# A 31-tap convolution split between VectorE and GpSimd: another order of its parts, and W_out in order of use

## What is computed

```python
z = rms_norm(x, norm1_g) @ w_in                      # 1024 -> 512 pool, 512 value, 512 gate
y_pool = einsum((window_mean(u) - u), pool_lin) * pool_scale   # 4 groups, windows 2, 4, 8, 16
v = a * sigmoid(gate)
h = depthwise_conv(v, width 31) + conv_dw_b          # causal, 512 channels
h = layer_norm(h, ln_g, ln_b);  y_conv = h * sigmoid(h)
x = x + concat(y_pool, y_conv) @ w_out + b_out
x = x + hier_moe(rms_norm(x, norm2_g))               # 32 experts, top 2 in the top group
y = rms_norm(x)
```

## Time and profile before

| | us |
|---|---|
| median of 3 runs (range) | 1133.28 (1131.29 to 1134.9) |
| the profiled execution | 1134.65 |
| its span, first to last instruction | 1132.9 |
| busy: PE | 944.6 |
| busy: DVE | 950.2 |
| busy: ACT | 622.2 |
| busy: POOL | 320.5 |

### The profile page before, as it was taken

How to read it: one execution, slowest core, us unless ns; L and a number is a source line. 1 busy time by engine, 2 the same in 40 slices (tenths; PEclk the granted TensorE clock), 3 DMA queues, 4 the chain that set the end, 5 groups by cost and what they waited for, 6 DMA issues and landing times.

```text
span 1132.9 us, 13497 instructions
## 1 busy us (share of the span) xinstructions
PE 944.6 (83%) x4446; PEld 774.3 (68%) x4446; DVE 950.2 (84%) x965; ACT 622.2 (55%) x596; POOL 320.5 (28%) x292
## 2 busy tenths in 40 slices
PE   4997887377469999497999999999999999999720
PEld 4786766254347887476888888888888888888510
DVE  6289999989987687788988989889898988989338
ACT  7213412116443421374788787878788788787323
POOL 2138969636652110112111111211112111111000
PEclk8998988688689999588999999999999999999865
DMA  8201100103004435268999999999999999999556
GB/s 252 94 20 37 38 19 19 56 1 118 1 19 149 183 115 195 80 230 293 383 380 381 386 383 394 394 388 393 376 391 375 384 379 378 384 382 348 206 233 248
DMA packets 66299, 268.63 MB, mean 237 GB/s; under 512 B 15215, under 2 KB 28015, under 8 KB 40601
## 3 DMA queue, kind: packets, MB, share of 16 engines
q1 hardware_dynamic: 56761, 250.36, 59.3%
q0 software_dynamic: 9504, 17.85, 4.1%
HBM read 254.09 MB, written 30.86 MB: 252 GB/s over the span
## 4 chain that ended last, share of the span: by engine, by line
PE 60%; DVE 25%; issue 3%; ACT 2%; DMA 1%; POOL 0%; DVEq 0%; POOLq 0%; ACTq 0%
DVE arena L1116 16%; PE ps L986 10%; PE ps L984 10%; PE ps L985 10%; PE ps L998 5%; PE ps L999 5%; PE ps L1000 5%; PE ps L973 3%; PE ps L774 2%; PE ps L775 2%; PE ps L776 2%; DVE arena L1424 2%; PE ps L1005 1%; DVE big L1157 1%; PE ps L918 1%
## 5 line engine op out<-in xcount | busy, mean ns | idle before, releaser
L699 ACT ACTIVATE big<-arena 128x2048 fp32r<-128x2048 f32 x192 | 362.6, 1913 | 70.5 <-PE ps L1000 36.4
L1359 DVE TENSOR_TENSOR low<-arena,big 128x2048 fp32r<-128x2048 f32 x126 | 285.1, 2284 | 39.9 <-ACT big L699 37.2
L1116 DVE SCALAR_TENSOR_TENSOR arena<-arena,cols 128x512 f32<-128x512 f32 (+2 forms) x210 | 226.7, 1134 | 1.9
L984 PE MATMUL ps<-big,ring 128*128 128x512 f32 x512 | 204.1, 399 | 2.4 <-DVE ring L1364 2.4
L986 PE MATMUL ps<-big,ring 128*128 128x512 f32 x512 | 202.0, 395 | 0.0
L774 PE MATMUL ps<-big,ring 128*128 128x512 f32 (+2 forms) x432 | 165.6, 383 | 40.5 <-DVE ring L1181 17.1
L1359 DVE TENSOR_TENSOR big<-arena,big 128x2048 fp32r<-128x2048 f32 x66 | 150.9, 2288 | 18.8 <-ACT big L699 15.4
L775 PE MATMUL ps<-big,ring 128*128 128x512 f32 (+2 forms) x432 | 163.3, 378 | 0.0
L776 PE MATMUL ps<-big,ring 128*128 128x512 f32 (+2 forms) x432 | 162.2, 376 | 0.0
L774 PEld LDWEIGHTS ps<-big,ring 128*128 128x128 f32 (+1 forms) x432 | 84.4, 195 | 56.9 <-issue 26.0
L984 PEld LDWEIGHTS ps<-big,ring 128*128 128x128 f32 x512 | 96.8, 189 | 22.0 <-DVE ring L1364 2.8
(11 more groups left out here) (217 smaller groups left out, 1287.2 us busy)
## 6 DMA issues: line engine op xcount, KB each, us to landing
arena<-in_w_eg SPq DMA_DIRECT2D x64, 1024.0 KB, 7.4
arena<-in_w_eu SPq DMA_DIRECT2D x64, 1024.0 KB, 7.0
arena<-in_w_ed SPq DMA_DIRECT2D x64, 1024.0 KB, 7.1
arena<-in_x_prompt SPq DMA_DIRECT2D x16, 512.0 KB, 5.3
y_in<-y_scratch SPq DMA_DIRECT2D x8, 1024.0 KB, 12.2
arena<-in_w_in SPq DMA_DIRECT2D x12, 512.0 KB, 3.5
arena<-in_w_out SPq DMA_DIRECT2D x8, 512.0 KB, 3.7
x_scratch<-arena SPq DMA_DIRECT2D x8, 512.0 KB, 2.8
```

Source lines behind the costliest of these rows:

```text
L699: act.activation(we_h[n % RING], raw[n % RING], ACT.Copy).then_inc(high_done, 1)
L984: pe.matmul(out, part_h[b][:, k, :], wh[:, q, :], start=(k == 0), stop=False)
L1116: dve.scalar_tensor_tensor(hc[:, c, a:b], v_ext[:, c, a + j:b + j], cols[:, c, j:j + 1], hc[:, c, a:b], ALU.mult, ALU.add).then_inc(conv_s ...
L1359: dve.tensor_tensor(we_l[n % RING], raw[n % RING], we_h[n % RING].bitcast(F32), ALU.subtract).then_inc(low_done, 1)
```

## The change

The parts are cut anew. DVE does A of all four tiles first, one after the other, then B of tile 2, B of tile 3 and C of tile 1; C is now the last 206 columns (from CUT = 912). POOL, with ACT's products in three buffers instead of two, adds the 606 later columns of tile 0 and 400 of tile 1, both during the in-projection, and nothing after it. There are three conv_done signals: after the A parts, after B3, after C1. All four pool chunks now stand behind the gate and value chunks.

The window scaling and the difference move from ACT and POOL to DVE, as one instruction per group; POOL's window sums wait for it where they reuse a buffer. The 64-column block of a chunk lies in bank 2 for both sets, so before it PE also waits until the chunk just before was read (taken(j - 1)). The first mean moves from chunk 11 to chunk 10, the first variance into chunk 11. The out-projection of a tile is cut in a half of convolution rows (out_conv) and one of pool rows (out_pool), W_out is loaded and split in that order (WO_ROWS), and the sample tokens of the pool product are a product of their own. PE's order becomes out_conv(0), out_conv(1), out_pool(0), out_pool(1), turn_hm(0), tile 2, the means, turn_hm(1), the variances, logits(0), tile 3. The name run stands for the same slice of hc as before.

```diff
-        KINDS = [("gate", 0), ("value", 0), ("gate", 1), ("value", 1), ("gate", 2), ("value", 2), ("pool", 3),
-                 ("gate", 3), ("value", 3), ("pool", 2), ("pool", 1), ("pool", 0)]
+        KINDS = [("gate", 0), ("value", 0), ("gate", 1), ("value", 1), ("gate", 2), ("value", 2), ("gate", 3),
+                 ("value", 3), ("pool", 3), ("pool", 2), ("pool", 1), ("pool", 0)]
...
-        CUT = HW_ - 220
-        PART = {"A": (0, BANK), "B": (BANK, HW_), "C": (BANK, CUT)}
-        HELPED = [(1, BANK, HW_), (3, CUT, HW_)]
-        help_n = {4: 7, 5: 7, 6: 7, 8: 6, 9: TAPS - 1 - 27}
-        DVE_WO = (0, 1, 4, 5, 6)
+        CUT = BANK + 400
+        PART = {"A": (0, BANK), "B": (BANK, HW_), "C": (CUT, HW_)}
+        HELPED = [(0, BANK, HW_), (1, BANK, CUT)]
+        help_n = {2: (0, 6), 3: (0, 7), 4: (0, 7), 5: (0, 7), 6: (0, 3), 7: (1, 10), 8: (1, 10), 9: (1, 10)}
+        WO_ROWS = list(range(NG, KD)) + list(range(NG))
+        DVE_WO = (0, 1, 2, 3, 4)
...
             for j in range(1, NCH):
                 pe.wait_ge(wl_done, j + 1)
                 if j >= 2:
+                    taken(j - 2)
                 for n in range(3):
+                    if n == 2:
+
+                        taken(j - 1)
                     in_proj(j, n)
...
             pool_lin_product(0)
             pool_lin_product(1)
-            pe.wait_ge(cen_done, 1)
             pe.wait_ge(lnsd_done, 1)
             turn_state(2)
+            pool_lin_product(2)
+            pe.wait_ge(yp_done, 2)
+            pe.wait_ge(wl_dve, NC)
+            out_conv(0)
+            pe.wait_ge(st_done, 3)
             turn_state(3)
-            pool_lin_product(2)
             pool_lin_product(3)
+            pe.wait_ge(yp_dve, 2)
+            pe.wait_ge(st_done, 4)
+            out_conv(1)
+            pe.wait_ge(wl_done, NCH + len(POOL_WO))
+            pe.wait_ge(wl_dve, len(DVE_WO))
+            out_pool(0)
+            pool_lin_sample()
+            out_pool(1)
...
             glu(0)
-            taps(21, ("A", 0), ("B", 0))
+            taps(TAPS, ("A", 0))
             glu(1)
-            taps(TAPS - 21, ("A", 0), ("B", 0))
-            taps(10, ("A", 1))
+            taps(TAPS, ("A", 1))
             glu(2)
-            taps(TAPS - 10, ("A", 1), ("A", 2))
-            taps(10, ("A", 2), ("B", 2))
+            taps(TAPS, ("A", 2))
             glu(3)
             taps(TAPS, ("A", 3))
...
+            taps(9, ("B", 2))
+            ln_center(0)
+            taps(5, ("B", 2))
+            difference(0)
+            taps(7, ("B", 2))
+            difference(1)
+            taps(8, ("B", 2))
+            difference(2)
+            taps(2, ("B", 2))
+            ln_normal(0)
+            for k in range(4):
+                wo_low(k)
+            mix_conv_low(0)
+            difference(3)
+            pooled(2)
+            mix_conv_low(1)
+            wo_low(4)
+            pooled(3)
+            mix_pool_low(0)
+            mix_pool_low(1)
+            taps(10, ("B", 3))
...
+                if t == 0:
+                    pooled_sample()
+                    taps(TAPS - 10, ("B", 3))
+                    dve.wait_ge(conv_step, steps[0])
+                    dve.engine_nop().then_inc(conv_done, 1)
+                    taps(10, ("C", 1))
                 if t == 1:
-                    mix_low(t + 2)
-                    ln_center(1)
-                    ln_center(2)
+                    taps(TAPS - 10, ("C", 1))
+                    dve.wait_ge(conv_step, steps[0])
+                    dve.engine_nop().then_inc(conv_done, 1)
```

More of the change, by code:

```diff
@@ L660, in hm_turned @@
                 act.activation(hmT[:, :, 0:ROWS[t]], x_ps[:, :, 0:ROWS[t]], ACT.Copy).then_inc(hmT_done, 1)
+            ln_swish(0)
+            mix_conv_high(0)
+            pooled(1)
+            mix_conv_high(1)
+            state_rows(2)
+            wo_high(4)
+            wo_high(5)
+            state_rows(3)
+            wo_high(6)
+            wo_high(7)
             act.wait_ge(yp_dve, NG - 2)
-            mix_high(0)
-            mix_high(1)
+            for t in (0, 1):
+                act.activation(part_h[t][:, 0:NG, :], u_ext[:, :, t * P:(t + 1) * P], ACT.Copy).then_inc(mh_done, 1)
             act.wait_ge(st_out, 64)
-            products(1, TAPS)
             for t in range(NT):
@@ L814, in ln_mean, with ln_variance @@
                 ins.then_inc(mean_done, 1)
+            def ln_variance(n):
+                w = BLOCKS[n][1]
+                pe.wait_ge(sq_done, n + 1)
+                for c in range(NC):
+                    ins = pe.matmul(var_ps[n][:, 0:w], mean_w[:, :], sq[n][:, c, 0:w], start=(c == 0), stop=(c == NC - 1))
+                ins.then_inc(var_done, 1)
             per_block = BANK // P
@@ L872, in _, with pool_lin_sample @@
-            ln_variance(0)
+                if i == 2:
+                    pe.wait_ge(yp_done, 1)
+                if i == 3:
+                    pe.wait_ge(yp_dve, 1)
+                for tok, w in BLOCKS[0:2]:
+                    ins = pe.matmul(z_seq[i % 2 if i < 2 else 0][:, tok:tok + w], plin[:, g, :],
+                                    u_ext[:, g, PS + tok:PS + tok + w], start=True, stop=True)
+                ins.then_inc(pl_done, 1)
+            def pool_lin_sample():
+                for g in range(NG):
+                    ins = pe.matmul(pd_ps[:, g, :], plin[:, g, :], u_ext[:, g, PS + SEQ + PS:UW], start=True, stop=True)
+                ins.then_inc(pl_done, 1)
@@ new lines, in out_part @@
+            def out_part(t, rows, first):
+                r = ROWS[t]
+                for half in range(2):
+                    c0 = half * BANK
+                    for k in rows:
+                        for i, (sh, mv) in enumerate(((part_h, wo_h), (part_h, wo_l), (part_l, wo_h))):
+                            ins = pe.matmul(out_ps[t % 2][0:r, c0:c0 + BANK], sh[t % 2][:, k, 0:r], mv[:, k, c0:c0 + BANK],
+                                            start=(first and k == rows[0] and i == 0),
+                                            stop=(not first and k == rows[-1] and i == 2))
+                return ins
@@ L873, in _, with out_conv, out_pool @@
+            def out_conv(t):
+                pe.wait_ge(mixc_low, t + 1)
+                if t >= 2:
+                    pe.wait_ge(x2_done, t - 1)
+                out_part(t, WO_ROWS[0:NC], True)
+            def out_pool(t):
+                pe.wait_ge(ml_done, t + 1)
+                out_part(t, WO_ROWS[NC:KD], False).then_inc(out_done, 1)
             pe.wait_ge(u_done, NG)
@@ L904, in turn_hm @@
                 else:
-                    pe.wait_ge(st_done, 4)
+                    pe.wait_ge(conv_done, 2)
                 for k in range(KD):
@@ L945, in _ @@
             for t in range(NT + 3):
-                if t < NT:
-                    out_proj(t)
-                if t == 1:
-                    pe.wait_ge(conv_done, 2)
+                if 2 <= t < NT:
+                    out_conv(t)
+                    out_pool(t)
+                if t == 2:
+                    pe.wait_ge(yp_dve, 3)
+                    pe.wait_ge(conv_done, 3)
                     pe.wait_ge(help_done, 2 * TAPS)
@@ L1289, in _ @@
                     ln_normal(2)
-                if t != 1 and t + 2 < NT:
-                    mix_low(t + 2)
+                if t + 2 < NT:
+                    mix_conv_low(t + 2)
+                    mix_pool_low(t + 2)
                 if 2 <= t < NT + 2:
```

293 lines of the change are left out of this document (126 added, 167 removed).

## The result

| | before | after |
|---|---|---|
| median, us (range) | 1133.19 (1131.29 to 1134.9) | 1162.9 (1162.28 to 1166.16) |
| after / before | | 1.0263, interval 1.024 to 1.0285 |
| span of the profiled execution | 1132.9 | 1161.8 |

The change makes the kernel 29.7 us slower. The page of the changed kernel, busy time and chain by line, beside the earlier trace rows: DVE has 16 us more, POOL 33 us less, and the taps (now line 1154) are 19% of the chain instead of 16%.

A forecast was written before the change was run, and what follows sets the result against it. DVE was taken to bound the kernel up to 333.70, PE after. DVE's stretches and a 24 us serial chain put tile 3 at 388, 25.6 later: 1134.65 becomes 1160.3, 1.4 less as median, 1159; own range 1148 to 1170.

The forecast's parts named there:

- The bound: Whole kernel: DVE sets the pace up to 333.70, then PE; the end moves as much as tile 3's start.
- (b): Rival: PE's order decides; out_conv(0) starts 11 us earlier and all follows, faster at 1122; chance 0.13.
- (c): Rival: the move changes nothing; lost interleaving and waits are won back by the earlier block, 1133; chance 0.06.
- (d): Rival: each GpSimd add costs DVE its whole recorded length, 41 us more, 1200; chance 0.04.
- Up to the end of part A: In-projection from 62: DVE's taps, glu and GpSimd holds sum to 172.0 us, first LayerNorm signal at 234.
- To the first out-projection: From 234: B2 taps, differences, holds and wo_low take 53.7 us; out_conv(0) at 288 instead of 299.08.
- To residual(0) and what is left: After out_conv(0): residual(0) at 316, tile 2 at 349, conv_done(3) at 366, taken as 364.
- the 2 us that I took off: conv_done(3): 366 lowered to 364, because the prices came out 2 us high on the stretch 249.8 to 333.7.
- The serial chain: From conv_done(3) to tile 3: means, LayerNorm, transposes, variances and logits in series, 24 us, tile 3 at 388.
- rival (a): Slower by less: 400-column adds cost 0.27 and the serial chain runs at the upper clock level, 1146; chance 0.22.

The follow-up runs named there:

- e5: Changed kernel, 64-column block of odd chunks in its own bank, PE's new wait for the chunk just before gone: 1165.73 us (1.0273).
- e1: Changed kernel, GpSimd's 30 adds of tile 1 made 8 columns wide instead of 400: 1145.98 us (1.0109).
- e2: Changed kernel, all 60 GpSimd adds (tiles 0 and 1) made 8 columns wide: 1116.66 us (0.9847).
- e4: Kernel before, without GpSimd's and ScalarE's help with taps; VectorE does all later columns of tiles 1 and 3: 1123.28 us (0.9918).
- e7: e4 with the low parts of in-projection chunks 2 to 11 made by VectorE instead of GpSimd: 1115.75 us (0.9854).
- e3: Changed kernel, B of tiles 2 and 3 done in turn before the first out-projection: 1158.36 us (1.0215).
- e9: Kernel before, VectorE takes over the window differences, one instruction each with the scaling: 1132.95 us (0.9993).
- e11: Changed kernel, PE does the variances of blocks 1 and 2 before turn_hm(1): 1159.8 us (1.0239).
- e8: Changed kernel without GpSimd's 60 adds and ScalarE's products; VectorE does B2 with B0, B3 with B1 in turn: 1145.65 us (1.0114).
- e6: Kernel before, each pair of tap chains done one after the other as single chains: 1147.38 us (1.014).

## Why the prediction was right

*The bound.* The measured 1162.9 lies near the forecast and far from what (b), (c) and (d) give. The statement that all is decided by when DVE's list is done held: e5 (PE's wait gone) changed nothing that can be told, and e1, e2, e4 and e7 (only holds or work of DVE changed) moved the time by 17, 46, 10 and 8 us where 17, 43, 10 and 8 were expected. e3 and e9 gave less than expected, 4.5 for 7 and 0.6 for 3.

*Up to the end of part A.* Forecast 172.0 us; glu(0) started 0.96 earlier than before in this execution, and the stretch behind it took 175.1 (61.1 to 236.2). By the first means of e1 and e2 the 60 adds cost 48.6 us of it where 43.2 was taken: the 606-column add 1.01 for 0.88, the 400-column add, of which no row was at hand, 0.61 for 0.56. All else came out 2.3 us cheaper than its prices, so that the sum is only 3 us out is in part luck.

*To the first out-projection.* 53.7 forecast, 52.3 measured (236.2 to the 288.50 of the row above). The difference on DVE, for which only bounds stood, takes 1.30 (four times, line 1201), and 1.4 was taken.

*To residual(0) and what is left.* DVE waits 3.19 us for pooled(3), then 2.87 for the root, then 1.54, as laid out; residual(0) at 316.20 for 316, tile 2 at 348.43 for 349 (DVE in order of time, [idle before]):

```profile
298.09 1.28 DVE L1210 TENSOR_SCALAR arena<-ps,cols 128x1024 f32<-128x1024 f32 x1 [3.19 <-PE ps L883]
...
316.20 1.22 DVE L1255 TENSOR_TENSOR arena<-ps,arena 128x1024 f32<-128x1024 f32 x1
...
322.63 20.50 DVE L1154 SCALAR_TENSOR_TENSOR arena<-arena,cols 128x606 f32<-128x606 f32 x21
...
353.75 11.89 DVE L1154 SCALAR_TENSOR_TENSOR arena<-arena,cols 128x206 f32<-128x206 f32 x21
```

The 21 taps of B3 with a bias add beside them took 20.5 (20.7 forecast), the 21 of C1 11.9 (11.9). conv_done(3) came at 365.7 where 364 was taken: the 2 us that I took off, since the prices had come out high on another stretch, should have stayed on. They were high there by the length of the pairs, of which the new list has none; that is a guess, no run tells it.

*The serial chain.* 24 us forecast, 23.3 measured (365.8 to 389.11), of which e11 shows 3 to be the order of the transposes and variances. Here too small errors cancel: until DVE could centre, the means took 5.4 instead of 6.9; hm_turned and turn_hm took 2.9 instead of 2. PE's granted clock was 0.72 in the means and 0.76 from 372.0 to 389.1, against 1.00 from 349.3 to 362.4 before, so the other half of rival (a), this chain at the upper level, did not come either.

*The rest.* The forecast of 1159 is 3.9 us below 1162.9: 1.1 at tile 3, 0.9 in the stage after it, 1.3 among the experts, whose stretch varied by 2.3 us (652.3 to 654.6) over all the kernels of this study, and the difference of profile and median.

What the change wanted, an earlier first block, it got: the mean 12.8 us and the first half tile 10.6 us earlier. The price stands on the same engine. In the experiments' terms, e8 against e4 puts the difference of the two orders at 22.4 us when nobody helps with the taps, and the help itself makes the other 7: it costs 17.3 us in the changed kernel and 10.1 before. Of the 22.4, single chains are about 14 by e6, on the kernel before. The rest lies in the order, with PE's idle stretch between tiles 1 and 2 and the serial chain (3 us of it by e11); how it adds up was not taken apart further.

## What to carry to other kernels

A list on one engine that is busy 99% of a stretch can be priced instruction by instruction, with the holds that another engine puts on it, and its end forecast to a few microseconds; a wait of an engine that is ahead is worth nothing, however long. Work given to GpSimd is a help to VectorE only if it takes less of VectorE's time than VectorE would need for it: take that price from the spacing of VectorE's instructions beside it, not from either engine's busy time. And where instructions of one chain wait for each other, run two chains in turn.

## What the runs showed of the hardware

**Help that costs more than it saves.** Beside one GpSimd instruction with its inputs in SBUF, a VectorE instruction with two such inputs is late by 0.98 to 1.01 (606 columns, e1 against e2) or 0.56 to 0.61 us (400 columns, e1). The same 606 columns done by VectorE cost 0.76 as part of a pair (16 taps in 12.16 us, e3) and 0.89 alone. In the kernel before an add of 606 beside a single chain costs 0.88, no more than that tap alone, so the gain of e4 rests in large part on running the taps taken over in pairs; no run separates the two. For a 1024-column subtraction it is 2.02 against 1.28 (e7). So all three pieces of GpSimd work moved to VectorE made the kernel faster or left it as it was: -10.1, -7.5, and -0.6 or -2.9 us.

**Behind pairs GpSimd can be kept out.** Behind pairs, whose instructions follow each other without a gap, one GpSimd subtraction was recorded with 19.3 us of the 22.07 in the earlier trace rows and one with 18.3; in e4, where VectorE runs more pairs, the nine have a mean of 7024 ns, with single chains 2624 (e6) and 2653 (changed kernel):

```profile
L1477 POOL TENSOR_TENSOR ring<-arena,ring 128x1024 fp32r<-128x1024 f32 x9 | 63.1, 7024 | 62.4 <-ACT ring L497 62.2 <-POOL fix L1515 0.2
```

Not every GpSimd instruction behind pairs was kept out: the adds in the kernel before took their turns there too (seven in 12.1 us from 98.38). What decides which way it goes was not found.
